# A fused two-block transformer kernel: the arena of buffers moves up by 64 bytes, to a multiple of 128

## What is computed

```
u = modulate(rmsnorm(h, norm1_g[l]), mod[:, 0, 0], mod[:, 0, 1])
h = h + FFN_RES_WEIGHT * mod[:, 0, 2][:, None, :] * swiglu(u, ffn1_w_gu[l], ffn1_w_down[l])
...
act = jax.nn.gelu(up[..., :D_FF]) * up[..., D_FF:]
x = x + jnp.einsum('bsf,fd->bsd', act, w_down[i])
```

## Time and profile before

| | |
|---|---|
| Median of 3 executions | 2085.08 us (2084.03 to 2087.66) |
| Profiled execution | 2083.68 us |
| Its span, first to last instruction | 2081.9 us |
| TensorE busy | 2043.3 us, 98% |
| VectorE busy | 1102.2 us, 53% |
| ScalarE busy | 806.2 us, 39% |
| GpSimd busy | 116.7 us, 6% |
| Mean granted TensorE clock | 0.995 |
| DMA traffic | 236.27 MB, 113 GB/s over the span |

### The profile page before, as it was taken

How to read it: one execution, slowest core, us unless ns; L and a number is a source line. 1 busy time by engine, 2 the same in 40 slices (tenths; PEclk the granted TensorE clock), 3 DMA queues, 4 the chain that set the end, 5 groups by cost and what they waited for, 6 DMA issues and landing times.

```text
span 2081.9 us, 25090 instructions
## 1 busy us (share of the span) xinstructions
PE 2043.3 (98%) x10215; PEld 1704.7 (82%) x10215; DVE 1102.2 (53%) x1681; ACT 806.2 (39%) x1252; POOL 116.7 (6%) x139
## 2 busy tenths in 40 slices
PE   5999999999999999999999999999999999999997
PEld 4788888888878898888888887778888888888887
DVE  8744544577753554333335646665425476346546
ACT  4322222345554343222323436555323353234334
POOL 3100000200000010000002000000000100000012
PEclk9999999999999999999999999999999999999999
DMA  7744433443423323233222332222332222332241
GB/s 276 249 166 162 167 139 133 159 141 116 144 96 102 91 68 116 76 104 114 86 73 89 120 122 72 73 81 91 101 98 95 72 102 82 110 102 95 70 149 41
DMA packets 71202, 236.27 MB, mean 113 GB/s; under 512 B 8864, under 2 KB 11168, under 8 KB 70704
## 3 DMA queue, kind: packets, MB, share of 16 engines
q1 hardware_dynamic: 68912, 226.59, 32.6%
q0 software_dynamic: 2032, 7.90, 1.2%
q10 hardware_dynamic: 144, 0.18, 0.0%
HBM read 229.89 MB, written 4.75 MB: 113 GB/s over the span
## 4 chain that ended last, share of the span: by engine, by line
PE 92%; DVE 3%; issue 2%; DMA 1%; ACT 1%; POOL 1%; DVEq 0%; SPq 0%; POOLq 0%; ACTq 0%
PE bank L676 81%; PE bank L740 4%; PE bank L1084 1%; PE bank L1070 1%; PE bank L966 1%; PE bank L857 1%; PE bank L860 1%; DMA w_raw<-in_w_gu_dram 1%; DVE raw_m L1633 1%; POOL ssq L2255 0%; PE bank L996 0%; DVE w_raw L1633 0%; PE bank L771 0%; DMA w_raw<-in_w_mix_dram 0%; PE bank L1116 0%
## 5 line engine op out<-in xcount | busy, mean ns | idle before, releaser
L1637 DVE TENSOR_TENSOR w_lo<-w_raw,w_hi 128x1024 fp32r<-128x1024 f32 (+2 forms) x367 | 418.4, 1168 | 204.2 <-ACT w_hi L1181 203.5
L676 PE MATMUL bank<-u_hi,w_hi 128*128 128x512 f32 (+1 forms) x1920 | 496.9, 372 | 9.8 <-ACT ple_s L1359 3.5
L676 PE MATMUL bank<-u_lo,w_hi 128*128 128x512 f32 (+1 forms) x1920 | 495.5, 371 | 6.2 <-DVE u_lo L1937 5.2
L676 PE MATMUL bank<-u_hi,w_lo 128*128 128x512 f32 (+1 forms) x1920 | 497.1, 371 | 0.0
L1181 ACT ACTIVATE w_hi<-w_raw 128x1024 fp32r<-128x1024 f32 (+2 forms) x368 | 347.6, 977 | 261.0 <-PE bank L676 196.1
L676 PEld LDWEIGHTS bank<-u_hi,w_hi 128*128 128x128 f32 x1920 | 357.3, 189 | 71.5 <-ACT ple_s L1359 3.9
L676 PEld LDWEIGHTS bank<-u_lo,w_hi 128*128 128x128 f32 x1920 | 357.6, 189 | 67.7 <-DVE u_lo L1937 5.8
L676 PEld LDWEIGHTS bank<-u_hi,w_lo 128*128 128x128 f32 x1920 | 358.0, 190 | 58.9
L1765 DVE TENSOR_TENSOR ff_a<-ff_s,bank 128x512 f32<-128x512 f32 x44 | 30.2, 687 | 223.9 <-issue 211.7
L1257 ACT ACTIVATE act_hi<-ff_a 128x512 fp32r<-128x512 f32 x66 | 41.8, 634 | 257.6 <-DVE ff_a L1765 217.6
L676 PE MATMUL bank<-act_hi,w_lo 128*128 128x512 f32 (+1 forms) x561 | 131.1, 379 | 0.0
(11 more groups left out here) (275 smaller groups left out, 2086.3 us busy)
## 6 DMA issues: line engine op xcount, KB each, us to landing
w_raw<-in_w_gu_dram SPq DMA_DIRECT2D x127, 512.0 KB, 4.1
w_raw<-in_w_ada_dram SPq DMA_DIRECT2D x66, 512.0 KB, 4.4
w_raw<-in_w_dn_dram SPq DMA_DIRECT2D x48, 384.0 KB, 3.1
w_raw<-in_w_mix_dram SPq DMA_DIRECT2D x36, 512.0 KB, 3.6
w_raw<-in_w_dn_dram SPq DMA_DIRECT2D x48, 320.0 KB, 3.2
w_raw<-in_w_in_dram SPq DMA_DIRECT2D x24, 512.0 KB, 3.6
w_raw<-in_w_o_dram SPq DMA_DIRECT2D x16, 512.0 KB, 3.4
w_raw<-in_w_in_g_dram SPq DMA_DIRECT2D x16, 512.0 KB, 3.5
```

The source lines that it names most:

```text
L676: m = e.matmul(bank[b][:, c], w, (x.lo if part == 2 else x.hi)[:, k, c], start=start, stop=stop, skip_group_check=True)
L1637: e.tensor_tensor(lo_of(name), raw_of(i), f32(hi_of(name)), ALU.subtract).then_inc(*s_w_lo.inc(name))
```

## The change

The arena's offset behind `base` is rounded up to 128 bytes and not to 64, and the sum of both is asserted to be a multiple of 128. In this build `arena` becomes 124288, and the arena's first byte 140800. Every buffer made by `ar` moves up by 64 bytes. `base`, what stands ahead of the constants, and the constants stay, and so do the two buffers that the attention keeps over constants that are no longer used (`at_pte`, `at_c0`). No instruction is added, removed or put elsewhere on any engine.

```
@@ -410,7 +410,9 @@
     negone_r = const("negone_r", [P, P], F32R)
     cact = const("cact_t", [P, D], F32)
-    arena = (cat + 63) // 64 * 64
+
+    arena = (cat + 127) // 128 * 128
+    assert (base + arena) % 128 == 0
     assert base + arena + 86 * KB + 32 <= nc.sbuf_usable_end, base + arena + 86 * KB - nc.sbuf_usable_end
```

## The result

The changed kernel is slower: 2092.78 us median of 5 executions (2091.06 to 2096.27) against 2084.19 us (2083.55 to 2087.66) of the kernel before beside it, ratio 1.004 [1.0025, 1.0054]. That is 8.6 us more, above the range of the prediction, which had looked for a gain.

A forecast was written before the change was run, and what follows sets the result against it. TensorE, busy 2043.3 of 2081.9 us, was taken as the bound. Terms -5.2 + 0.9 - 0.2 + 0.2 + 0.4 + 0.3 - 0.1 = -3.7 us took the 2085.08 us median to 2081.4 us; range 2079.0 to 2086.0 us.

The forecast's parts named there:

- the sum's first term: Line 676, 512 columns, moving operand in the arena: 2349 matmuls go from 228.9 to 226.67 ns, gaining 5.2 us.
- The pairing that seemed to part them: Attention, both operands in the arena: two 512-column matmuls at 235 ns each, taken to speak for the start itself.
- The one called slower: TensorE: distance between moving operand and weights goes from 64 to 128 modulo 256, costing 2.2 ns each; 2090 us, chance 0.05.
- The rival of no change by the place above 137 KB: Arena matmuls: the 2.2 ns belong to the upper memory, not the start; time stays 2085.0 us, chance 0.20.
- The one of more gain: Arena matmuls: 256 columns keep their advantage and narrow ones don't lose; about 2079.5 us, chance 0.16.
- the term of +0.9 us: Line 676, 256 columns, moving operand in the arena: 390 matmuls go from 117.7 to 120.0 ns, losing 0.9 us.
- The 16-byte lines: Memory cachelines: 64 and 128 are both multiples of 16, so by that rule nothing changes, 2085.0 us.
- The 4% on the first tiles: DMAs into the arena: cutting descriptors at 256-byte boundaries would make the 14 first tiles 4% shorter by estimate.
- The counts: Line 676, moving operand in the arena: 2349 matmuls of 512 columns and 390 of 256.
- TensorE's idle time: Sign: if `act` steps by 226.7 ns but the span doesn't follow, idle time, 38.6 us, grows by as much.
- the other engines and the DMAs: Arena accesses off TensorE: other engines expected 0, upper bound 0.2 us; DMA transfers 0.1 us of gain.
- The term for the narrow matmuls of the attentions: Both attentions: 128-column matmuls lose 0.4 us by columns plus 32; two-pass f32 ones taken as 0.3 us loss.

The follow-up runs named there:

- the kernel with the arena at 256: Kernel before with the arena's offset behind `base` rounded up to a multiple of 256 (124416); 2075.17 us against 2082.15, ratio 0.9964.

## Why the prediction was wrong

**The step that failed** is the premise of the sum's first term: "After the change the arena is at 124288, and every arena buffer starts at a multiple of 128, like `u` does today." The multiple of 128 was true and had no say; what `u` has and the arena doesn't is its distance of 0 to the weights. Before the change the distance was 64, after it 128, and I read "like `u`" off the wrong quantity. The term of -5.2 us for the 2349 matmuls became +10.4. Moving everything together (no effect) and moving the weights under a `u` that stays (the classes change sides) show this; it isn't only argued. Why a distance costs what it costs, no run shows.

**Why the trace allowed it.** It held two classes, and in both the start modulo 128 and the distance modulo 256 differ in step. Two classes can't part the two. The pairing that seemed to part them was that of the attention's scores, with both operands in the arena, so at a distance of 0 modulo 256, and yet 235 ns. It was no evidence. The same pair in the kernel with the arena 192 bytes up, where the moving operands of the arena are fast:

```profile
575.88 0.39 PE L857 MATMUL bank<-qs,ks 128*128 128x512 f32 x1
576.11 0.39 PE L860 MATMUL bank<-qs,kla 128*128 128x512 f32 x1
576.34 1.77 PE L676 MATMUL bank<-u_hi,w_lo 128*128 128x512 f32 x7
```

It still takes 0.46 us for two. These are lone steps between other sizes and other weights, shown to 10 ns, and something else holds them above 226.7 ns; what, wasn't tried. I had set a pace from two steps against paces from 176 and 208.

**The rivals.** The one called slower named the mechanism, the distance going from 64 to 128 modulo 256, and its point of decision, 231 ns; its chance of 0.05 was too low for a mechanism that the rows could not part from the favoured one, and its price of 2.2 ns, 2090 us, was half of the 4.4 ns measured. The rival of no change by the place above 137 KB is false: at a distance of 0 the same place is as fast as `u`. The one of more gain, in which the narrow matmuls keep their advantage, was half right by accident: after the change they kept 1.3 ns of the 2.3, and the term of +0.9 us is +0.4.

**The two cited passages.** The 16-byte lines of the Trainium skill (SBUF — State Buffer, Specifications) were to change nothing between multiples of 64; by that rule this kernel would have stayed at 2084 us, and the trace disagrees, with 233.3 against 228.9 ns. The 4% on the first tiles, estimated from the whole beats of the Trainium skill (DMA: Bandwidth & Descriptors, How a descriptor splits into AXI transactions), don't show. From 4 to 18 us the DMAs moved 395 GB/s before and 400 in the changed kernel, but 393 in the kernel with `base` 64 bytes up, whose arena starts at the very same 256-byte boundary; so the small difference doesn't go with the start. The first `act` began 0.7 us later, not earlier, beside a lower granted clock (below).

**What held.** The counts, and with them the accounting: 390 and 2349 times the measured differences reproduce the stages. `u` stayed at 226.6 ns, TensorE's idle time didn't grow (38.6 to 37.6 us), and the other engines and the DMAs added nothing to the path. The term for the narrow matmuls of the attentions, 0.4 + 0.3 us, wasn't measured by itself. The gain that was forecast is there for whoever goes to a distance of 0: five kernels with it measured 0.9968, 0.9964, 0.9964, 0.9965 and 0.997, on the mean 0.9966, about 7 us less than before. The counted matmuls explain 2349 x 2.25 - 390 x 2.1 ns = 4.5 us of these; each interval by itself reaches down to some 4 to 5 us, but five that agree leave little to chance, and the source of the other 2.5 us is open. One candidate shows in the last item below: in four of the five profiles the first `act` began 3.3 to 4.0 us earlier than before, beside a higher granted clock.

## What to carry to other kernels

Place the moving operands of long matmuls (512 columns here) and the buffers that their weights are loaded from in the same class modulo 256 bytes, which is easiest if every region begins at a multiple of 256 behind a common base; here that is worth 0.35%, while a rounding to 128 cost 0.4%. A trace with two classes says that something separates them, not what: list every quantity that differs between the two (own start, place, distance to each operand read beside it) and weigh the change by each of them, above all by one under which it lands in a class that has no row. Read a matmul's pace from start times over at least some ten groups; its mean duration moved by 3 to 4 ns where the pace moved by 4.4, and a step between two single matmuls decides nothing: in the kernel before, single steps of `act` go round 229, 232 and 226 ns, and in the changed kernel those of `ga` alternate between 238 and 229.

## What the runs showed of the hardware

- A 32-bit matmul of 128 by 128 weights takes 544 cycles for 512 columns with moving operand and weights at the same offset modulo 256 bytes, 549 with the moving operand 64 ahead, and 560 at 32, 128, 192 and 224. These are means of stretches in which all matmuls have the same distance, at a granted clock of 1.00. Why 64 alone is mild isn't settled.
- With 256 columns the order turns: 288 cycles at a distance of 0 (119.8 to 120.0 ns), 272 at 192 (113.5 ns), the others between. The long ones lose and the short ones gain by the same distance; no run explains it. A distance of 192 would be the better one for a kernel that has only matmuls of 256 columns, an estimate from these two paces; with `w_lo` alone at 192 its narrow groups took 117.8 ns.
- The price goes with a matmul's own weights, not with those loaded beside it, and has an aftereffect: behind a `w_lo` group at a distance of 192 the first six matmuls with `u_lo` step by 228.1 to 236.0 ns although they are at 0 themselves, and from the second on those before and behind them too; then it is 226.5. Matmuls that change between distances can cost more than at either one (line 740: 232.0 ns, against 226.7 at 0 and 229.0 at 64).
- The start of the first `act` stage scatters between executions with the granted clock of the first 100 us. The window from 60 to 100 us of the kernel with the arena at 256, whose first `act` begins at 166.96 us, and of the changed kernel, 170.99 us:

```profile
60.00:100.00 40.00, 38.01 (x167) 30.84 (x166) 27.04 (x36) 17.22 (x22) 5.61 (x8) 1.00 0.73 252
```

```profile
60.00:100.00 40.00, 37.05 (x150) 29.74 (x149) 26.00 (x35) 17.20 (x22) 5.60 (x8) 0.91 0.72 250
```

  The clock of 1.00 against 0.91 (0.96 in the kernel before, 170.29 us) goes with 167 against 150 matmuls in the same 40 us. It isn't tied to the distance alone: the kernel with the arena 448 bytes up has distance 0, a clock of 0.96 and starts `act` at 169.66 us, the one with it 128 up has 192, a clock of 1.00 and starts at 166.78. But of the fourteen kernels profiled six had a clock of 1.00 in this window, and four of the six are among the five with both `u` and the arena at distance 0; of the other nine two had it. One execution of each can't say whether that is chance. The start of the first `act` ranges from 166.3 to 172.1 us, which is a good part of the scatter of single executions; what decides the clock there is open.
